# Two encoder layers on one core: the end of each layer in one block, with the residual stored feature by token

## What is computed

```python
yp = yp + mp                                   # mp = mixer features (2048) @ w_out
yp = yp + memory_attend(rms_norm(yp, mnorm_g[l]), mk_p, mv_p, w_mq, mq_g, w_mo)

def memory_attend(h, mk, mv, w_mq, mq_g, w_mo):
    q, z = _split(h @ w_mq, (M_W, M_W))        # 4 heads x 128 each
    q = rms_norm(q.reshape(n_b, L, M_HEADS, M_HD), mq_g)
    o = _softmax_attend(q, mk, mv, None, None) # over 256 memory tokens
    return (o.reshape(n_b, L, M_W) * jax.nn.silu(z)) @ w_mo
```

## Time and profile before

| | us |
|---|---|
| median of three runs | 3903.7 (3902.22 to 3903.99) |
| the profiled execution | 3896.49 |
| its span, first to last instruction | 3894.8 |
| TensorE busy | 3631.9 (93%) |
| VectorE busy | 1118.3 (29%) |
| ScalarE busy | 1104.3 (28%) |
| GpSimd busy | 466.8 (12%) |
| mean granted clock of TensorE | 0.964 of 2.4 GHz |

### The profile page before, as it was taken

The page is one execution under the profiler, slowest core; times in us unless marked ns, Lnnn a source line. Parts: engine busy times, 40 slices in busy tenths (PEclk is TensorE's granted clock), DMA queues, the critical chain, the costliest instruction groups (busy, mean ns, idle before and its releaser), DMA issues. The chain is left out here.

```text
span 3894.8 us, 46760 instructions
## 1 busy us (share of the span) xinstructions
PE 3631.9 (93%) x16220; PEld 2509.8 (64%) x16220; DVE 1118.3 (29%) x2751; ACT 1104.3 (28%) x2773; POOL 466.8 (12%) x473
## 2 busy tenths in 40 slices
PE   6799999998799999999899988999999999699988
PEld 3377777776577777777544564677777777444564
DVE  1235555555323333333200023012222211201022
ACT  1333333333233333333201133022222222201140
POOL 0044444444100000000000000000000000000000
PEclk9799999999799999999999999999999999799999
DMA  5112231112022232211323004111111110423003
GB/s 158 46 29 35 35 34 34 34 29 29 25 39 39 41 43 42 38 42 33 126 68 120 23 14 142 45 33 36 46 46 46 41 41 16 151 66 123 23 12 123
DMA packets 238329, 208.89 MB, mean 54 GB/s; under 512 B 24679, under 2 KB 211975, under 8 KB 238167
## 3 DMA queue, kind: packets, MB, share of 16 engines
q1 hardware_dynamic: 224606, 178.79, 19.2%
q10 hardware_dynamic: 13568, 28.07, 1.9%
HBM read 158.01 MB, written 48.82 MB: 53 GB/s over the span
## 5 line engine op out<-in xcount | busy, mean ns | idle before, releaser
L1001 PE MATMUL gdn_pj<-hT,Wb 128*128 128x352 f32 x1536 | 514.0, 461 | 2.9 <-DVE gdn_OI L1445 2.9
L2272 PE MATMUL gla_pj<-hT,Wb 128*128 128x352 f32 x1536 | 470.0, 460 | 2.2 <-PEq L2132 1.6
L1739 PE MATMUL band_pj<-hT,Wb 128*128 128x384 f32 (+1 forms) x1152 | 386.6, 465 | 13.0 <-DVE band_tick L2060 10.0
L2272 PEld LDWEIGHTS gla_pj<-hT,Wb 128*128 128x128 f32 x1536 | 290.5, 190 | 151.2 <-issue 2.9
L563 PE MATMUL out_Y<-out_W,out_oS 128*128 128x512 f32 (+1 forms) x864 | 373.7, 592 | 0.0
L1001 PEld LDWEIGHTS gdn_pj<-hT,Wb 128*128 128x128 f32 x1536 | 266.2, 192 | 91.8 <-DVE gdn_OI L1445 3.0
L563 PEld LDWEIGHTS out_Y<-out_W,out_oS 128*128 128x128 f32 (+1 forms) x864 | 156.7, 181 | 214.1 <-issue 214.1
L1739 PEld LDWEIGHTS band_pj<-hT,Wb 128*128 128x128 f32 x1152 | 207.3, 193 | 94.9 <-DVE band_tick L2060 10.4
L2268 PE MATMUL gla_pj<-gla_Wv,hT 128*128 128x256 f32 x1152 | 264.9, 380 | 0.0
L289 PE MATMUL mem_pj<-hT,finish_Wq 128*128 128x352 f32 x768 | 235.3, 466 | 3.0 <-PEq L45 3.0
L2268 PEld LDWEIGHTS gla_pj<-gla_Wv,hT 128*128 128x128 f32 x1152 | 217.6, 190 | 29.6
(11 more groups left out here) (382 smaller groups left out, 4997.2 us busy)
## 6 DMA issues: line engine op xcount, KB each, us to landing
Wb<-in_l_w_in_dram SPq DMA_DIRECT2D x96, 512.0 KB, 7.9
out_oS<-o_features SPq DMA_DIRECT2D x16, 1024.0 KB, 5.8
out_W<-in_l_w_out_dram SPq DMA_DIRECT2D x6, 2048.0 KB, 15.3
o_features<-gla_OF ACTq DMA_DIRECT2D x16, 528.0 KB, 5.5
mkv_W<-in_l_w_mkv_dram SPq DMA_DIRECT2D x2, 4096.0 KB, 25.3
x_prompt<-out_xS ACTq DMA_DIRECT2D x16, 512.0 KB, 5.5
finish_Wq<-in_l_w_mq_dram SPq DMA_DIRECT2D x8, 1024.0 KB, 8.6
mo_xS<-x_prompt SPq DMA_DIRECT2D x16, 512.0 KB, 3.4
```

The source lines that it names most:

```text
L1001: mm = pe.matmul(pj[:, m % 2, 0:w], W[:, j, k, :], hT[:, k, c0:c0 + w], start=k == 0, stop=k == KD - 1)
L1739: mm = pe.matmul(out[:, 0:w], W[:, j, k, :], hT[:, k, c0:c0 + w], start=k == 0, stop=k == KD - 1)
L2272: mm = pe.matmul(pj[:, m % 2, 0:w], W[:, SLOT[kind], k, :], hT[:, k, c0:c0 + w], start=k == 0, stop=k == KD - 1)
```

## The change

The residual is now kept as features by tokens, in DRAM and in SBUF. The first norm becomes turn_input: it turns the input tiles, stores them as features by tokens, sums the squares over features with a matrix of ones on TensorE, and writes hT.

project_out and memory_attend are gone. finish_layer is one block, without barriers inside. The output projection keeps a 128 x 128 block of w_out as stationary operand and streams the features of 1056 tokens in parts of 384, 384 and 288. The first two groups of output features (n = 0, 1) go block by block of input features, as these arrive; the others n by n. VectorE adds the residual, ScalarE squares, GpSimd adds up the squares, and one matmul with ones for each part sums them over partitions. The queries are projected next. The gates and the second projection are no stages of their own any more: they are a stream of single matmul steps (STREAM: 96 steps of gates, 96 of the second projection, and in layer 0 three sums for the next norm), from which fill(k) takes k steps at a time between the attention's own instructions. A unit of attention is now two heads of a tile, 18 units; each iteration takes three, three and two steps. In layer 1 the result is turned back by transposes at the end.

```diff
-def memory_attend(nc, name, ident, ones, eps, hT, W, w_ld, mq_g, kv_prompt, kv_sample, o_dram):
...
-def project_out(nc, name, ident, eps, kt, w_out, parts, o_dram, x_in, x_out, gain, hT, ahead=()):
...
+def turn_input(nc, ident, ones, eps, x_in, xT_dram, gain, hT):
...
+                for t in range(TILES):
+                    src = x_in[1] if t == TILES - 1 else x_in[0][128 * t:128 * t + 128, :]
+                    sp.dma_start(xS[0:rows(t), t, :], src).then_inc(x_ld[t], 16)
+                sp.dma_start(g[:, :], gain.rearrange("(k p) -> p k", p=128), allow_slow_non_contiguous=True).then_inc(g_ld, 16)
+                for t in range(TILES):
+                    sp.wait_ge(copied, t + 1)
+                    sp.dma_start(xT_dram.rearrange("(k p) t -> p k t", p=128)[:, :, cols(t)], xT[:, :, cols(t)]).then_inc(st, 16)
+                sp.wait_ge(st, TILES * 16)
...
+                def total(t):
+                    pe.wait_ge(squared, t + 1)
+                    wait(pe, rooted, t - 1)
+                    for k in range(KD):
+                        mm = pe.matmul(PS[:, t % 2, 0:rows(t)], ones[:, :], sq[:, t % 2, k, 0:rows(t)], start=k == 0, stop=k == KD - 1)
+                    mm.then_inc(summed, 1)
+
+                for t in range(TILES):
+                    r = rows(t)
+                    pe.wait_ge(x_ld[t], 16)
+                    wait(pe, squared, t - 1)
+                    for k in range(KD):
+                        mm = pe.transpose(TP[:, t % 2, k, 0:r], xS[0:r, t, 128 * k:128 * k + 128], ident[0:r, 0:r])
+                    mm.then_inc(turned, 1)
+                    if t:
+                        total(t - 1)
+                total(TILES - 1)
...
+                    act.wait_ge(turned, t + 1)
+                    act.activation(xT[:, :, cols(t)], TP[:, t % 2, :, 0:r], ACT.Copy).then_inc(copied, 1)
+                    wait(act, summed, t - 1)
+                    act.activation(sq[:, t % 2, :, 0:r], TP[:, t % 2, :, 0:r], ACT.Square).then_inc(squared, 1)
+                    if t:
+                        root(t - 1)
...
+                    for k in range(KD):
+                        mm = dve.scalar_tensor_tensor(hT[:, k, cols(t)], xT[:, k, cols(t)], g[:, k:k + 1], rs[:, t % 2, 0:r],
+                                                      ALU.mult, ALU.mult)
+                    mm.then_inc(h_out, 1)
...
+def finish_layer(nc, l, ident, ones, eps, hT, Wb, out_ld, w_out, w_mq, w_mo, mnorm_g, mq_g, o_dram,
+                 x_in, x_out, y_out, next_gain, kv_prompt, kv_sample, ahead):
+
+    KT_, UN = 16, 2 * TILES
+    PARTS = [(0, 384), (384, 384), (768, 288)]
...
+        FIRST, FILL = (4, 4), (3, 3, 2)
+        PER = sum(FILL)
+        STREAM = [("z", c, h) for c in range(3) for h in range(M_H)]
+        for c in range(3):
+            STREAM += [("m", c, n) for n in range(KD)]
+        if next_gain is not None:
+            for c in range(3):
+                at = STREAM.index(("m", c + 1, 2)) if c < 2 else len(STREAM)
+                STREAM.insert(at, ("s", c, 0))
+        LEN = {"z": KD, "m": M_H, "s": 1}
+        ends = [sum(LEN[kind] for kind, _, _ in STREAM[:i + 1]) for i in range(len(STREAM))]
...
+                for k in range(KT_):
+                    sp.dma_start(oT[:, k, :], o_rows[:, k, :]).then_inc(o_ld[k], 16)
+                load_ahead(sp, [out_weights(slots[n], w_ld[n], w_out, n) for n in (2, 3)])
+                for n in range(KD):
...
+                for k in range(KT_):
+                    pe.wait_ge(o_ld[k], 16)
+                    for n in range(2):
+                        for c, (c0, w) in enumerate(PARTS):
+                            mm = pe.matmul(ps[:, 3 * n + c, 0:w], slots[n][:, k, :], oT[:, k, c0:c0 + w], start=k == 0, stop=k == KT_ - 1)
+                            if k == KT_ - 1:
+                                mm.then_inc(y_done, 1)
+                for n in range(2, KD):
+                    pe.wait_ge(w_ld[n], 16)
+                    for c, (c0, w) in enumerate(PARTS):
+                        pe.wait_ge(x_new, 3 * (n - 2) + c + 1)
+                        for k in range(KT_):
+                            mm = pe.matmul(ps[:, 3 * (n % 2) + c, 0:w], slots[n % 4][:, k, :], oT[:, k, c0:c0 + w],
+                                           start=k == 0, stop=k == KT_ - 1)
+                        mm.then_inc(y_done, 1)
+                        if n == KD - 1 and c:
+                            total(c - 1)
+                    if n in (2, 3):
+                        turn_keys(0, n - 2)
...
+                            before, bc, bx = STREAM[i - 2]
+                            if before == "z":
+                                pe.wait_ge(z_out, 4 * bc + bx + 1)
+                            elif before == "m":
+                                pe.wait_ge(m_new, 8 * bc + bx + 1)
+                            else:
+                                pe.wait_ge(m_ln, bc + 1)
...
+                for u in range(2):
+                    scores(u)
+                    fill(FIRST[u])
+                for u in range(UN + 1):
+                    if u < UN:
+                        turn(u)
+                    fill(FILL[0])
+                    if u + 2 < UN:
+                        scores(u + 2)
+                    fill(FILL[1])
+                    if u:
+                        values(u - 1)
+                    fill(FILL[2])
...
+                    for t in range(6):
+                        pe.wait_ge(m_new, 8 * (t // 3) + 8)
+                        if t >= 3:
+                            pe.wait_ge(y_a, t - 2)
+                            pe.wait_ge(y_d, t - 2)
+                        turn_y(t, range(KD)).then_inc(y_turn, 1)
+                        fill(M_H)
...
+                        if x == M_H - 1:
+                            act.wait_ge(z_out, 4 * c + 4)
+                            act.activation(ZS[:, :, part_of(c)], ZS[:, :, part_of(c)], ACT.Silu).then_inc(z_ok, 1)
+                            act.preload_act_table_set("natural_log_exp_and_others")
...
+                for u in range(UN):
+                    jobs(steps_at(u))
+                    copy_turned(u)
+                    jobs(steps_at(u) + FILL[0])
+                    if u + 2 < UN:
+                        soften(u + 2)
...
+                    elif kind == "s":
+                        dve.wait_ge(z_done, 12)
+                        dve.wait_ge(m_rs, c + 1)
+                        dve.wait_ge(m_new, 8 * c + 8)
+                        normal(c, 1, rs2[c % 2], m_h)
...
+                for u in range(UN + 1):
+                    jobs(steps_at(u))
+                    if u + 1 < UN:
+                        weigh(u + 1)
+                    jobs(steps_at(u) + FILL[0])
+                    if u + 2 < UN:
+                        peak(u + 2)
+                    jobs(steps_at(u) + FILL[0] + FILL[1])
+                    if u:
+                        out(u - 1)
...
-        project_out(nc, "norm0", ident, eps, 0, None, (), None, x_in, None, l0_norm_g, hT)
+        turn_input(nc, ident, ones, eps, x_in, xT[0], l0_norm_g, hT)
```

845 lines of the change are left out of this document (475 added, 370 removed).

## The result

| | before | after |
|---|---|---|
| median | 3902.98 us (3902.22 to 3903.99, 4 runs) | 3768.98 us (3768.53 to 3773.04, 4 runs) |
| ratio | | 0.9658, 95% interval 0.9644 to 0.9673 |
| the profiled execution | 3896.49 | 3768.96 |

The kernel is 134 us (3.4%) faster. In three later sessions the kernel before had medians of 3902.9, 3903.7 and 3904.7 (single runs from 3899.0 to 3908.4). In the last of them the changed kernel, run again, had 3769.62.

A forecast was written before the change was run, and what follows sets the result against it. The prediction took TensorE, busy 93% of the span, as the bound: columns streamed plus its stops. Gains of 70.6 (layer 0) and 61 (layer 1) less 5 (turn_input) made 127 us off the 3903.7 median: 3777, range 3760 to 3813.

The forecast's parts named there:

- Price of a column: TensorE's matmul records, start to start: 0.834 ns a column and 2 ns a record, so 384 columns cost 0.3226 us.
- Rival (d): In the two projections, narrow matmuls don't hide their weight loads: 2 x 62 us come back, 3902, no change; chance 0.01.
- Layer 0: The end of layer 0, from its first transfer to GLA's first matmul: 475 us against 545.5, a gain of 70.6.
- The end of the queries: Behind the query projection, the last square sum needs ScalarE and VectorE: 2.5 us idle and 2 more for the clock.
- Layer 1: The end of layer 1, from its first transfer to the span's end: 472 us against 532.8, a gain of 61.
- Attention: One attention iteration (two heads of a tile) takes TensorE 7.3 us with eight fill steps, which hide its chain.
- Rival (a): Attention fill hides only part; gate activations and streamed norms fall on TensorE in full: 34 us back, 3811; chance 0.14.
- Rival (c): Attention runs in lockstep, its chain not hidden: 3.7 us for each of 38 iterations, 139 us, 3916; chance 0.03.
- turn_input: The stage in place of the first norm: 38 us for nine tiles, 5 more than before; bounds -2 and +17.
- Rival (b): turn_input runs with TensorE at the lower clock: +12 on the forecast, 3789; chance 0.10.
- The sum of 127: Whole kernel: gains of 70.6 in layer 0's end and 61 in layer 1's, less 5 for turn_input, 127 us less.
- off the median this gives 3777: Last step, whole kernel: the 127 us taken off the median of three runs, 3903.7, giving 3777; chance 0.70.

## Why the prediction was right, and where it was off

**Price of a column.** Right: 0.83 ns, 96 records in 28.40 us (28.4 said), and +50.8 for the columns given back (51). Rival (d) is out. The rule of the Trainium skill that the prediction weighed (TensorE: Matmul & The Clock Gate, Back-to-back issue gap) doesn't hold for these fp32 streams: 96 columns more in a record, at the same number of records, cost the full 80 ns. These columns and the cover in the attention (+28 without it) are what runs show of the 134 us. The rest, some 55 us of old norms, transposes, barriers and their waits, is read from the traces; no run puts them back one by one.

**Layer 0**, 472.1 against 475. The first wait was 3.5 (3.4 said). The end of the queries had 2.1 idle; the 2 us for the clock weren't spent, as the clock was 1.00 through the whole attention. Stalls of the streamed normalisation: 0.7 + 2.7 + 0.3 was said, and there was one, of 2.1. The tail was 11.2 (2360.5 to 2371.7) against 12.9. These are 5.7 us less; TensorE's own work and start were 2.8 more than my sum. Without that second miss the stage would have been further off.

**Layer 1**, 472.2 against 472: the tail was 10.1 for 9.7 and the end of the queries had 2.1 idle for 4.5, so here too TensorE's own work was some 2 us more than my sum, and the two cancel by chance.

**Attention.** The period is 7.36 (7.3 said), no idle at all. Rival (a), that activations and normalisations fall on TensorE in full, is out for this kernel: even ScalarE held twice as long costs nothing, and of the streamed norms 2.1 us fell on it. Rival (c) had the right mechanism at the wrong size: without fill the units do run in lockstep with the chain, but at 2.58 us and not at 2.2 + 3.7, since two units are in flight. It would never have reached 139 us (38 x 3.7 is 140.6, to be exact); the run without any fill lost 28.

**turn_input** is the term that was missed in place: +5 was said, +0.2 measured. TensorE's clock was 0.90 on average in this stretch where the first norm had 0.50, and a tile went at ScalarE's pace, 2.65 us, not 3.2; VectorE waited 17 us for its gain vector and then caught up at 0.26 us an operation. Windows of the old and of the new stage from start to last write, before and then after the earlier trace rows:

```profile
86.94:120.88 33.94, 16.74 (x72) 13.47 (x72) 11.55 (x19) 22.85 (x36) 0.00 (x0) 0.50 0.39 128
```
```profile
88.19:122.34 34.15, 25.89 (x216) 25.14 (x216) 18.37 (x72) 22.40 (x37) 0.00 (x0) 0.90 0.82 255
```

Rival (b) is out. The clock rose here in a stretch that is transposes and short sums by turns. The sentence of the Trainium skill (TensorE: Matmul & The Clock Gate, Part 4) that transposes don't count as activity would have kept it low by the prediction's use of it; with the sums in between, this row can't refute it for transposes alone.

**From the profile to the median.** The sum of 127 stands against 127.7 between the two profiled executions. That sum is right partly by luck: turn_input took 5 us less than said, and the band 6 more. And I subtracted it from the median of the runs before, which lies 7.2 us above the profiled execution (3903.7 and 3896.49); all other runs of that kernel, in four sessions, took 3899.0 or more. After the change the profiled execution lies at the median. So the step that failed is "off the median this gives 3777": I carried those 7 us over as if they were spread over the whole kernel. By the profiled execution the forecast would have been 3896.5 - 127 = 3769.5, and the time was 3769.0. Where the other executions of the kernel before spend their 7 us has no trace. The band's stall, which is 3.7 us there and up to 17 in kernels with the same band, could explain it; this is argued, not shown.

## What to carry to other kernels

Before independent matmuls are laid into a chain as cover, work out the chain's own period (here 2.58 us for two heads) and the pure work (2.2): cover above the difference buys no speed, but room. Here half of it gave all of the time, and the whole of it lets ScalarE stop for 8 us without loss. Price a stop of TensorE at more than its length, since the clock was low behind each (here 2 to 3 us more a stop of 3 to 8 us). And where two kernels differ by 5 to 15 us of 3800, ask first whether a stage that neither changed has moved: compare its length and its "issue" waits, at the jumps of its loops first, before giving the difference to the edit. A sum of terms read from one execution belongs to that execution's time.

## What the hardware showed that I had not expected

- Adding 40 to 64 idle instructions an engine made the kernel 8.4 us faster, adding 100 on three engines made it 15.2 slower, 6.3 of these by their own length and most of the rest by code fetched anew in every pass of DeltaNet's loop (23 instruction transfers where the other kernels have none).
- A stop of TensorE of 3 to 8 us, in dense work, left the granted clock of the following stretch at 0.91, 0.83 and 0.79, and cost 2 to 3 us on top of its length.
- GpSimd's square of 1024 elements took 1.9 us mostly and 6.25 across a dense run of VectorE, which it outlasted by 1.75; a small operation of VectorE beside a square took up to 2.00 us for 0.34.
- A record's duration can't be added up along a chain: two exponentials with their reads show 1.33 us of durations and take 0.91.
